# Compression of the cache pages: transposes of the next unit issued inside the present unit's products, first differences taken per sequence

## The reference, cut to what matters

```python
def _compress(kraw, w1, b1, w2, b2, pe):
    ...
    ch = kp.reshape(B, n_ch, CMP_STRIDE, NSA_KV_HEADS, HEAD_DIM)
    w1r = w1.reshape(CMP_RATIO, CMP_STRIDE, HEAD_DIM, CMP_HIDDEN)
    parts = jnp.einsum('bnsgd,rsdh->rbngh', ch, w1r)
    n_cmp = n_ch - CMP_RATIO + 1
    h = parts[0, :, 0:n_cmp]
    for r in range(1, CMP_RATIO):
        h = h + parts[r, :, r:r + n_cmp]
    h = h + (pe.reshape(-1) @ w1) + b1
    out = jax.nn.gelu(h) @ w2 + b2
```

## Time and profile before

| what | value |
|---|---|
| median of the runs shown | 2244.59 us (2244.12, 2244.59, 2252.13) |
| the profiled execution's own time | 2242.59 us |
| its span | 2240.8 us |
| mean granted clock of TensorE | 0.978 |
| busy: PE, DVE, ACT, POOL | 95%, 50%, 35%, 40% |
| the compression's products, start to end | 192.9 to 450.5 us |

### The profile page before, as it was taken

The page is one execution under the profiler, slowest core; times in us unless marked ns, Lnnn a source line. Parts: engine busy times, 40 slices in busy tenths (PEclk is TensorE's granted clock), DMA queues, the critical chain, the costliest instruction groups (busy, mean ns, idle before and its releaser), DMA issues. The chain is left out here.

```text
span 2240.8 us, 37919 instructions
## 1 busy us (share of the span) xinstructions
PE 2122.5 (95%) x15414; PEld 1875.2 (84%) x15414; DVE 1115.9 (50%) x2002; ACT 791.1 (35%) x1594; POOL 893.2 (40%) x620
## 2 busy tenths in 40 slices
PE   5998999999999989997899999899999999999998
PEld 3997787855777689987799999678999999997886
DVE  5114323254766720259631045666876665664558
ACT  3203222134566621336522131234333333333553
POOL 2322222120111231212321124164388788776786
PEclk8999999998999999998999999999999999999999
DMA  7564434274110051100223130221245344357872
GB/s 265 195 219 153 178 119 150 87 277 167 32 32 11 1 142 38 38 8 3 69 67 95 38 113 20 100 88 65 71 148 178 123 146 165 123 183 272 272 230 104
DMA packets 152757, 268.20 MB, mean 120 GB/s; under 512 B 17817, under 2 KB 86348, under 8 KB 147975
## 3 DMA queue, kind: packets, MB, share of 16 engines
q1 hardware_dynamic: 144375, 222.70, 29.8%
q0 software_dynamic: 8208, 43.07, 5.5%
HBM read 211.93 MB, written 58.08 MB: 120 GB/s over the span
## 5 line engine op out<-in xcount | busy, mean ns | idle before, releaser
L3448 PE MATMUL PS<-down_parts 128*128 128x512 f32 x924 | 213.3, 392 | 0.1
L3448 PEld LDWEIGHTS PS<-down_parts 128*128 128x128 f32 x924 | 174.2, 189 | 38.0 <-issue 0.9
L3405 PE MATMUL PS<-part_hi,w_ring 128*128 128x258 f32 x1152 | 192.2, 285 | 0.0
L3405 PEld LDWEIGHTS PS<-part_hi,w_ring 128*128 128x128 f32 x1152 | 161.8, 191 | 4.6 <-issue 4.6
L3405 PE MATMUL PS<-sum_blocks,w_ring 128*128 128x258 f32 x1296 | 160.1, 284 | 0.9 <-DVE out_sums L3971 0.9
L3405 PEld LDWEIGHTS PS<-sum_blocks,w_ring 128*128 128x128 f32 x1296 | 158.3, 190 | 1.2 <-DVE out_sums L3971 1.2
L643 POOL TENSOR_TENSOR w_merge_parts<-w_merge_raw,w_merge_parts 128x1024 fp32r<-128x1024 f32 x24 | 59.5, 2503 | 202.5 <-ACT w_merge_parts L636 202.5
L3797 POOL TENSOR_TENSOR down_parts<-down_raw,down_parts 128x512 fp32r<-128x512 f32 x71 | 117.4, 1667 | 45.6 <-ACT down_parts L3603 45.2
L2343 PE MATMUL PS<-h_hi,w_merge_parts 128*128 128x344 f32 x768 | 131.4, 323 | 0.0
L2343 PEld LDWEIGHTS PS<-h_hi,w_merge_parts 128*128 128x128 f32 x768 | 122.0, 188 | 3.1 <-issue 3.0
L1809 ACT ACTIVATE scores<-scores,mins_p 128x640 f32<-128x640 f32 (+5 forms) x192 | 112.4, 588 | 28.0 <-DVE mins_p L1851 27.2
(11 more groups left out here) (599 smaller groups left out, 5161.3 us busy)
## 6 DMA issues: line engine op xcount, KB each, us to landing
down_raw<-act_blocks SPq DMA_DIRECT2D x77, 256.0 KB, 3.4
w_or_ada<-w_ada SPq DMA_DIRECT2D x8, 2048.0 KB
w_raw<-w_up SPq DMA_DIRECT2D x11, 1024.0 KB, 9.4
w_raw<-w_gate SPq DMA_DIRECT2D x11, 1024.0 KB, 6.7
w_down_rows<-w_down SPq DMA_DIRECT2D x11, 1024.0 KB, 7.3
w_down_blocks<-w_down_sums SPq DMA_DIRECT2D x11, 1024.0 KB, 9.0
down_raw<-w_down_blocks SPq DMA_DIRECT2D x44, 256.0 KB, 4.2
act_blocks<-act_sums SPq DMA_DIRECT2D x10, 1024.0 KB, 5.1
```

What stands on the lines that cost most here:

```text
L3405: last = pe.matmul(out[:, c, :], r32(w[:, k, :]), r32(h[:, k, QUART * c:QUART * c + QUART]), start=first and k + i == 0, stop=k == 3 and i ...
L3448: last = pe.matmul(PS[:, t, c], r32(s[:, x, P * (t % 4):P * (t % 4) + P]), r32(s[:, y, c]), start=first and i == 0, stop=last_j and i == 2 ...
```

## The change

PE no longer turns the whole of unit u+1 ahead of `layer1(u)`. The first item of unit u+1 is turned in the first half of `layer1(u)`, between its second product (L1072) and the middle one (L1077). The second item is turned at the start of the second half, ahead of its `late_rows` if it has any. The waits for the present unit's differences stay ahead of the first half. DVE takes the first difference of an item right after its copies of that item, instead of both differences after the copies of both items.

```diff
+            def later_item(u, n):
+
+                if u + 1 < NU:
+                    for k in units[u + 1][2][n:n + 1]:
+                        transposes(pe, items[k])
+
             def layer1(u):
...
-                pe.wait_ge(d1_done, mine[-1] + 1)
-                pe.wait_ge(d2_done, mine[-1] + 1)
-                pe.wait_ge(w_in[which], 16)
-                pe.wait_ge(pe_ready, which + 1)
                 for hh in range(2):
                     col = slice(P * hh, P * hh + P)
+                    if hh == 1:
+                        later_item(u, 1)
+                    else:
+                        pe.wait_ge(d1_done, mine[-1] + 1)
+                        pe.wait_ge(d2_done, mine[-1] + 1)
+                        pe.wait_ge(w_in[which], 16)
+                        pe.wait_ge(pe_ready, which + 1)
                     if u in late_at and hh == late_half(u):
                         late_rows(late_at.index(u))
...
                     for j in range(8):
                         pe.matmul(PS[:, 4 + hh, M3:M3 + n3], wt[:, 8 + j, col], X[:, u % 2, 2, j, 0:n3], start=j == 0, stop=j == 7)
+                    if hh == 0:
+                        later_item(u, 0)
                     pe.wait_ge(sum_ready, which + 1)
...
             for u in range(NU):
-                if u + 1 < NU:
-                    for k in units[u + 1][2]:
-                        transposes(pe, items[k])
                 layer1(u)
...
             for k in read_chunks(v, 1, odd_read):
                 u = items[k][0]
+                if u in FIRST:
+                    bias_columns(units[u][0])
+                first_difference(k)
                 if k == units[u][2][-1]:
-                    if u in FIRST:
-                        bias_columns(units[u][0])
-                    for x in units[u][2]:
-                        first_difference(x)
                     if u:
```

## The result

The changed kernel takes 2257.18 us (median of 20 executions, 2250.29 to 2263.95); the kernel before, timed beside it, takes 2245.11 us (20 executions). The ratio is 1.0057, 95% interval 1.0047 to 1.0066: 12 us slower, about twice the 5.8 us forecast, and just above the upper end of the range.

What follows compares the result with a forecast made beforehand. PE, busy 95% of the span, was taken as the bound. Shifts of +3.7 us through unit 5, +1.8 in unit 6 and +0.2 in units 7 and 8 made +5.8, so 2250 us; range 2240 to 2257.

Steps and rivals of the forecast that it cites:

- (a): Transposes of a pair, split by item: 2.45 us per item, 4.90 instead of 5.29 per pair, gaining 0.4 us per unit.
- (b): Late rows in units 2, 3, 4, 7, 8: the wait for DVE's `late` loses its cover, 0.5 us each, 2.4 in all.
- the sum: Whole kernel: the shifts over the units add up to 5.8 us, or 0.26% slower.
- (c): Differences per item, POOL then DVE: PE stands 3.1 us ahead of `layer1(1)` and 2.1 us ahead of `layer1(6)`.
- (d): Stage start: `layer1(0)` waits only for the prompt's difference and starts at 189.0, 3.9 us earlier.
- (e): Moved gathers and late rows' weight loads: they still land in time, 8.4 us against 12.5 available, costing nothing.
- a rival: PE's clock falls after the new idle stretches: 2252 to 2260 us; chance 18%, of which 11 points for over 2256.
- The price of one fall: PE after an idle stretch: the lower clock for most or all of 4 us loses 1.7 to 2 us.
- the dearest single fall of the prediction: PE after an idle stretch: a clock fall that lasts twice as long costs 4 us.
- The argument against the rival: Against a clock fall at units 1 and 6: PE works without a gap ahead of the second and third standing.

Runs made afterwards that it cites:

- short units left as before: Changed kernel, but the prompt's units 0 and 5 turn the whole next pair ahead of their products and DVE's order is as before: 2245.65 us, ratio 1.0000.
- unit 0 filled: Changed kernel with 4 dead matmuls (results unused) where PE idles ahead of `layer1` of unit 0 only: 2255.10 us, ratio 1.0048.
- the filled kernel: Changed kernel with dead matmuls where PE idles: 4 ahead of `layer1` of unit 0, 3 ahead of unit 1, 2 ahead of unit 6: 2252.98 us, ratio 1.0030.
- DVE's order as before: Changed kernel, PE's order kept, but both first differences again come after the copies of both items: 2252.11 us, ratio 1.0036.
- unit 1 filled: Changed kernel with 3 dead matmuls (results unused) where PE idles ahead of `layer1` of unit 1 only: 2256.82 us, ratio 1.0060.
- the stand alone: Kernel before, with PE also waiting 4 us for the prompt's first difference before turning unit 1's pages: 2243.64 us, ratio 0.9996.
- groups of three: Changed kernel with a pair's eight transpose groups placed three, three and two, DVE's order as before: 2235.44 us; with two dead matmuls at the start 2232.32 us.

## Why the prediction was wrong

**(a) The pair, split: right.** An item takes 2.45 us and its fourth group waits for ACT, as in rows 3 and 4. That splitting as such neither costs nor gains shows in the kernel with the short units left as before (1.0000).

**(b) The late rows' wait: right in size, incomplete.** 0.38 us idle on `late` in units 2, 3, 4, 7 and 8, as in rows 6. Not in the sum: behind `late_back`, whose matmuls are small, the clock fell at unit 2 in four of the seven traces with an uncovered wait there, and the rows took 3.3 to 3.6 us instead of 1.85.

**(c) The chain from POOL to DVE: right.** The stand ahead of unit 1 was forecast at 3.1 us and is 3.13 where the clock is at 1.00 (unit 0 filled). Ahead of unit 6 it was forecast at 2.1 and is 2.05 in the two traces without a fall in unit 5.

**(d) The start: right for the engines**, `layer1(0)` at 188.98 for 189.0.

**(e) The DMAs: right.** No wait on the late rows' weights or a gather shows in the stage.

**The sum: right without the clock.** 5.8 forecast (its terms as printed add to 5.7), 5.9 in the filled kernel's trace.

**The step that failed is the clock: the sum puts it at nothing**, and left it to a rival whose chance and price were both too low. What it cost in fact is the difference between 5.8 us and the measured 12 (8.7 us in the profiled execution). The chance was 18%, though the prediction had PE stand for 4 us behind a few transposes. The clock fell behind that stand in each of the five traces that have it (the changed kernel twice, DVE's order as before, unit 1 filled, and the stand alone). The price of one fall was read from rows 7 as 1.7 to 2 us, the loss within stretches of 4 us that I had cut myself; nothing in those rows said that the fall ends where the stretch ends. At 46 to 50 us it does. The stretch of 1025 to 1029 was cut out of a fall of over 10 us, with PE busy in most of it, so a long one could have been read before the prediction (columns as in rows 2, kernel before):

```profile
1022.00:1033.00 11.00, 9.37 (x133) 8.57 (x132) 10.83 (x15) 6.16 (x11) 0.00 (x0) 0.53 0.00 1
```

Over 11 us that is 5.2 us lost, where the dearest single fall of the prediction costs 4. In the four traces in which short products follow the stand of 4 us the clock stays at half for over 10 us of PE's work, and in the three of them with DVE's new order `layer1(1)` starts 28.1 us after the stage's start, 4.3 later than with unit 0 filled. And a slower PE hands on its delay: the transposes at half clock made POOL's difference 1 us late, which is part of the 4.3. In the profiled execution the stage is 14.5 us longer, 8.7 more than the 5.8 forecast: 4.3 of these at unit 0, 2.4 in the first product of unit 1, and the other 2.0 in unit 5.

The argument against the rival, that PE works without a gap ahead of the second and third stands, is refuted for the second: with unit 0 filled the clock fell behind it although PE had been busy at 1.00 up to it. Busy there meant short products.

**What stays open.** In two of the six traces with the change's order in unit 5 (the changed kernel's first and the one with unit 1 filled) the clock fell there during short products, with no stand ahead. It did so in none of the traces in which a whole pair of transposes precedes that unit's products, nor in those in groups of three. No run isolates it. Nor does one show by itself that it is the short products that keep the clock down for over 10 us. The pairs of traces only agree with it: back after 4 to 5 us of work over transposes, after 10 to 12 over short products with an item of transposes among them. A run that puts wide products behind the same stand of 4 us would have told more. Nor does the length of a stand decide by itself: the same 2.3 us in the kernel before brought the clock down in three traces of four.

## What to carry to other kernels

Moving work from a place where it covers a wait needs the question "what does the engine do there now", and on TensorE a stand can cost more than its length: the half clock goes on over the work behind it. How much that is depends on what stands there: the same 4 us cost about 1 us more ahead of transposes and 4.3 ahead of the short products. Where a stand can't be avoided, a few dead matmuls in it can be worth more than they cost (4 us here, with all three stands filled). And a split should follow the resource that makes the groups wait: with three banks, groups of three; by items of four, each still waits.

## What the runs showed of the hardware

The granted clock fell in the stand of 4 us in five traces of five, 1 to 2 us after PE had stopped, so before the stand was over. With the prompt's short products ahead it fell behind stands of 2.0 to 3.1 us in five places of five and behind one of 1.63 us, and didn't behind 1.58, 1.38 and 0.62. Ahead of short products with transposes between, two waits of 0.89 and 1.41 us close together were enough in the one trace that has them (groups of 3, 3 and 2). It stayed at half for 10 to 12 us while PE was busy without a gap, over products of 128x65 and 128x63 and the transposes between them; with the same products and no stand ahead it stayed at 1.00. An engine that shows 100% busy in the profile can thus be running at half speed: the clock column has to be read beside the busy column.
